# Dilated attention: products in pairs of units by seven block products, logits ahead of the products in each step

## The reference, cut to what matters

```
x = x + rms_norm(gmlp_mixer(rms_norm(x, pre[0])), post[0])
h = rms_norm(x, pre[1])
z = h @ w_in                      # q, k, v of 3 groups x 16 heads x 64, and a gate of 1024
for g, dilation in enumerate((1, 4, 16)):
    logits = q[g] @ k[g].T / 8 + bias      # each query sees keys at offsets 0, +-d .. +-64 d
    m, p, den = max, exp(logits - m), sum
    o[g], lse[g] = (p / den) @ v[g], m + log(den)
y = sum over g of softmax(lse)[g] * o[g]
x = x + rms_norm((y * silu(gate)) @ w_out, post[1])
```

## Time and profile before

| | |
|---|---|
| time, median of 3 runs | 3752.05 us (3745.39 to 3757.55) |
| the profiled execution | 3743.86 us, span 3742.3 us |
| PE busy | 3590.3 us (96%) |
| DVE busy | 1977.6 us (53%) |
| ACT busy | 1312.6 us (35%) |
| attention, from gmlp's last products to its own turns | 729 to 784 us |
| the 24 turns | from 784 us on; one of groups 0 and 1 takes 51.4 us, one of group 2 45.2 us |

### The profile page before, as it was taken

The page is one execution under the profiler, slowest core; times in us unless marked ns, Lnnn a source line. Parts: engine busy times, 40 slices in busy tenths (PEclk is TensorE's granted clock), DMA queues, the critical chain, the costliest instruction groups (busy, mean ns, idle before and its releaser), DMA issues. The chain is left out here.

```text
span 3742.3 us, 48660 instructions
## 1 busy us (share of the span) xinstructions
PE 3590.3 (96%) x18034; PEld 2903.4 (78%) x18034; DVE 1977.6 (53%) x3847; ACT 1312.6 (35%) x2559; POOL 112.2 (3%) x137
## 2 busy tenths in 40 slices
PE   8999999899999999999998899999978999999999
PEld 6878887777777777777777687777976877888887
DVE  5387773353334445555555544544675667754443
ACT  4254443333323333333223434444323323232222
POOL 0000001000000000000000100000000000000000
PEclk9999999999999999999999999999989999999999
DMA  4222226411111112111111330111323322233333
GB/s 147 91 102 97 93 89 217 146 62 50 59 59 58 54 59 62 58 49 47 48 46 51 113 110 24 43 43 64 101 92 100 102 82 82 77 113 99 96 96 121
DMA packets 140884, 308.87 MB, mean 83 GB/s; under 512 B 31936, under 2 KB 70384, under 8 KB 140576
## 3 DMA queue, kind: packets, MB, share of 16 engines
q1 hardware_dynamic: 123904, 264.81, 22.0%
q0 software_dynamic: 14688, 33.22, 3.0%
q10 hardware_dynamic: 2112, 8.39, 0.6%
HBM read 256.55 MB, written 56.04 MB: 84 GB/s over the span
## 5 line engine op out<-in xcount | busy, mean ns | idle before, releaser
L142 DVE TENSOR_TENSOR all_w_lo<-all_w_raw,all_w_hi 128x1024 fp32r<-128x1024 f32 x295 | 361.1, 1224 | 337.8 <-ACT all_w_hi L137 337.7
L137 ACT ACTIVATE all_w_hi<-all_w_raw 128x1024 fp32r<-128x1024 f32 x295 | 310.1, 1052 | 478.9 <-PE om_z L155 261.2
L1465 PE MATMUL da_z<-all_hi,all_w_hi 128*128 128x512 f32 x736 | 305.7, 415 | 4.1 <-DVE all_w_lo L142 4.1
L1465 PE MATMUL da_z<-all_hi,all_w_lo 128*128 128x512 f32 x736 | 291.1, 396 | 0.0
L1465 PE MATMUL da_z<-all_lo,all_w_hi 128*128 128x512 f32 x736 | 289.8, 394 | 0.0
L1326 ACT ACTIVATE da_pt<-da_tr 128x512 f32<-128x512 f32 (+1 forms) x192 | 101.0, 526 | 485.7 <-PE da_tr L1518 485.7
L155 PE MATMUL om_z<-all_hi,all_w_hi 128*128 128x512 f32 x640 | 257.3, 402 | 7.9 <-DVE all_w_lo L142 4.7
L1334 ACT ACTIVATE at_p<-at_logit,da_pair_max 128x256 f32<-128x256 f32 (+1 forms) x384 | 178.0, 465 | 239.1 <-DVE da_pair_max L1720 238.7
L155 PE MATMUL om_z<-all_hi,all_w_lo 128*128 128x512 f32 x640 | 255.8, 400 | 0.0
L155 PE MATMUL om_z<-all_lo,all_w_hi 128*128 128x512 f32 x640 | 253.7, 396 | 0.0
L155 PE MATMUL pr_g<-all_hi,all_w_hi 128*128 128x344 f32 (+1 forms) x624 | 211.7, 339 | 10.7 <-issue 4.9
(11 more groups left out here) (692 smaller groups left out, 7781.0 us busy)
## 6 DMA issues: line engine op xcount, KB each, us to landing
all_w_raw<-in_w_mlp SPq DMA_DIRECT2D x128, 512.0 KB, 3.5
all_w_raw<-in_w_ug SPq DMA_DIRECT2D x48, 512.0 KB, 4.1
all_w_raw<-in_w_qkv SPq DMA_DIRECT2D x48, 512.0 KB, 3.7
all_w_raw<-in_w_in SPq DMA_DIRECT2D x27, 512.0 KB, 3.6
da_w_raw<-in_w_qkv SPq DMA_DIRECT2D x24, 512.0 KB, 3.6
all_w_raw<-in_w_bo SPq DMA_DIRECT2D x24, 512.0 KB, 3.5
all_w_raw<-in_w_v SPq DMA_DIRECT2D x20, 512.0 KB, 4.6
vhat<-ag_vst ACTq DMA_DIRECT2D x4, 2048.0 KB, 7.3
```

The lines of the kernel that those rows point to most:

```text
L137: self.nc.scalar.activation(self.hi[b][:, :], self.raw[b][:, :], ACT.Copy).then_inc(self.hi_done[b], 1)
L142: self.nc.vector.tensor_tensor(self.lo[b][:, :], self.raw[b][:, :], self.hi[b][:, :].bitcast(F32), ALU.subtract).then_inc(self.lo_done[b], 1)
L1465: last = nc.tensor.matmul(z[h][:, :], wp[u][:, ws], ap[:, kk, cols], start=(kk == 0 and m == 0), stop=(kk == KT - 1 and m == 2))
```

## The change

- **Products.** Units go in 38 pairs: q and k of a turn, v of two turns, two units of the gate. Class `Seven` makes a pair as 7 blocks of 12 products each (`ORDER`, `PRODUCTS`), 84 where two units had 96. The first four units (q and k of pair 0, v of pairs 0 and 1) stay as they were (192 products).
- **Weights of a block.** a11, a12, a21, a22 are 128 x 512 quarters of the pair's weights, each loaded by a DMA of its own; s1 to s4 are sums of them (DVE: `add_lower`, `add_left`, `add_three`, `add_four`). Each of the seven is split into one of four ring slots, three blocks ahead of its use: `split_hi(n+3)` on ACT waits until block n-1 has been multiplied, `split_lo(n+3)` on DVE waits for it.
- **Combination.** Four PSUM banks bx, by, bz, bv hold block products. ACT copies bx and bz to `n2`, `n3` and writes the first quarter; DVE forms n2, n3 and the other three quarters, of q, k and v in strided order.
- **`block_work(n)`.** On DVE it is `split_lo(n+3)` and, by n mod 7: 4: `add_lower`, `add_left`, n2, n3 and quarter c22; 5: c21; 6: `add_three`; 0: `add_four` and c12; 1, 2, 3: nothing more. It stands in the step in which block n begins, ahead of DVE's copies of v (s = 0) and its bias pass. On ACT it stands ahead of the copy of the turned p and the exponentials.
- **Order on PE.** Of a step the logits of tile s-1 come first, then the products, then transposes of p, then p times v. The v transposes of s = 0 stand behind the first half-block. The logits of tile 0 wait for DVE's v copies too.
- **Shares.** Steps get half-blocks of 6 products: `full`, 21 a turn; turn 1 `short`, 21 with 8 in its step 0; turn 24 two in each step; 25 half-blocks follow the turns.
- **Norm and copies.** h is normalised before it is multiplied, so no quarter is scaled by `inv` on leaving PSUM; q and k have two buffers and are not copied. `tr` and `pv` have one PSUM bank each instead of two.
- **Start.** The first half of tokens of the new x, its norm, and its split are made in gmlp's out phase (`next_x`, `next_square`, `next_norm`, `next_hi`, `next_lo`); the other half in attention.
- **Other moves.** Biases are loaded at s = 9 of the turn before; the results of group 2 go to DRAM by POOL as those of group 1 do, and come back after the turns, where `turn_y` now runs; the gate's tanh and product follow there. Loops are written out instead of run with registers.

```diff
...
+                if KT + 1 <= n < KT + 5:
+                    for k in range(2 * (n - KT - 1), 2 * (n - KT)):
+                        next_x(k)
+                        if k:
+                            next_total(k)
+                if n >= KT + 6:
+                    for k in range(4 * (n - KT - 6), 4 * (n - KT - 5)):
+                        next_norm(k)
+                    next_lo(n - KT - 6)
...
+class Seven:
+    ORDER = ("a11", "s3", "s1", "s2", "a22", "a12", "s4")
+    N = 7
...
+    def load(self, sp, j, part, unit):
+        before = self.N * (j - 1)
+        wait(sp, self.lo_done, before + {"a21": 2, "a11": 4, "a22": 5, "a12": 6}[part])
+        if part in ("a11", "a12"):
...
+    def add_lower(self, dve, j):
+        t = self.tile
+        self.landed(dve, j, "a21")
+        self.landed(dve, j, "a22")
...
+    def add_left(self, dve, j):
+        t = self.tile
+        self.landed(dve, j, "a11")
+        dve.wait_ge(self.summed, 4 * j + 1)
+        self.plus(t["s3"], t["a11"], self.scales[j], t["a21"]).then_inc(self.summed, 1)
...
+    def split_hi(self, act, n):
+        j, i = divmod(n, self.N)
+        name = self.ORDER[i]
+        if name in self.loaded:
...
+        else:
+            act.wait_ge(self.summed, 4 * j + {"s1": 1, "s3": 2, "s2": 3, "s4": 4}[name])
+        wait(act, self.multiplied, n - self.slots + 1)
+        self.nc.scalar.activation(self.hi[n % self.slots], self.tile[name], ACT.Copy,
+                                  scale=self.scales[j] if name in ("a11", "a12") else 1.0).then_inc(self.hi_done, 1)
+    def split_lo(self, dve, n):
...
+    def products(self, out, n, block, start, ks):
+        b = n % self.slots
+        for k in ks:
+            cols = slice(k * P, k * P + P)
+            for m, (wp, ap) in enumerate(((self.hi, block[0]), (self.lo, block[0]), (self.hi, block[1]))):
+                last = self.nc.tensor.matmul(out, wp[b][:, cols], ap[:, k, :], start=start and k == 0 and m == 0,
+                                             stop=k == KT // 2 - 1 and m == 2, skip_group_check=True)
+        return last
...
+        PRODUCTS = (("b11", bx, True), ("t3", bz, True), ("t1", bv, True), ("t2", by, True), ("t4", bz, False), ("b21", bx, False), ("b22", bv, False))
...
+        full, short = (2, 2, 2, 2, 1, 2, 2, 1, 2, 2, 1, 2), (8, 2, 2, 1, 1, 1, 1, 1, 1, 1, 1, 1)
+        share_of = {n: short if n == 1 else (2,) * SUB if n == turns else full for n in range(1, turns + 1)}
+        at, work = 0, {}
+        for n in range(1, turns + 1):
+            for s in range(SUB):
+                work[n, s] = range(at, at + share_of[n][s])
+                at += share_of[n][s]
...
+            for n in range(1, turns + 1):
+                for s in range(SUB):
+                    for blk in begun(work[n, s]):
+                        block_loads(blk)
...
+            def block_work(n):
+                if n + 3 < NB:
+                    seven.split_hi(act, n + 3)
+                j, r = divmod(n - 1, Seven.N)
...
+                if r == 0:
+                    wait(act, s_c12, j)
+                    act.wait_ge(seven.multiplied, n)
+                    nc.scalar.activation(n2, bx[:, :], ACT.Copy).then_inc(s_xc, 1)
+                if r == 1:
...
+                if r == 5:
+                    free_to_leave(act, j, 0)
+                    act.wait_ge(seven.multiplied, n)
+                    out, view = dest(j, 0, 0)
+                    nc.scalar.activation(out, view(bx[:, :]), ACT.Copy).then_inc(s_c11, 1)
...
+                    nc.scalar.activation(den[:, 0, :, :], den[:, 0, :, :], ACT.Ln).then_inc(s_dln, 1)
                 for s in range(SUB):
-                    if bg and s == 0:
...
+                    for blk in begun(work[n, s]):
+                        block_work(blk)
+                    if 3 <= s < 3 + tiles:
...
-                        nc.scalar.activation(pt[t % 2][:, 0:wd], tr[t % 2][:, 0:wd], ACT.Copy).then_inc(s_pt, 1)
-                    if ag is not None and 1 <= s < 1 + tiles:
...
+            def gemm(x):
+                n, half = divmod(x, 2)
+                j, i = divmod(n, Seven.N)
+                name, out, start = PRODUCTS[i]
+                if half == 0:
+                    pe.wait_ge(seven.lo_done, n + 1)
+                    if i < 4 and j == 0:
...
+                    for sem, count in (((s_c11, j),), ((s_c21, j),), ((s_c12, j),), ((s_n2, j),), ((s_zc, j + 1),), ((s_xc, j + 1),), ((s_c22, j + 1),))[i]:
+                        wait(pe, sem, count)
...
+                last = seven.products(out[:, :], n, blocks[name], start, range(2 * half, 2 * half + 2))
+                if half == 1:
+                    last.then_inc(seven.multiplied, 1)
...
-                        turn_y(n - 2 - B_PAIRS, tiles * n)
                     if 1 <= s < 1 + tiles:
...
-                            pe.wait_ge(s_qs, n)
-                            if bg == 2:
...
                         wait(pe, s_max, c)
                         k0 = t * P + (WINDOW if ag == 2 else 0)
...
-                            last = nc.tensor.matmul(qk[hh][:, 0:wd], q[hs, t * P:t * P + P],
-                                                    k_[hs, k0:k0 + wd], start=True, stop=True)
+                            last = nc.tensor.matmul(qk[hh][:, 0:wd], q[a % 2][hs, t * P:t * P + P],
+                                                    k_[a % 2][hs, k0:k0 + wd], start=True, stop=True)
                         last.then_inc(s_qk, 1)
+                    for x in work[n, s][0:1 if s == 0 else None]:
+                        gemm(x)
+                    if s == 0:
+                        values_ready(pe, a)
+                        wait(pe, s_pt, tiles * a)
...
+                            last = nc.tensor.transpose(dst[:, (m % 4) * P:(m % 4) * P + P], v_new[a % 2][:, off + m * P:off + m * P + P], ident)
+                        last.then_inc(s_vt, 1)
+                        for x in work[n, s][1:]:
+                            gemm(x)
...
-                        wait(pe, s_pt, c - 1)
+                        wait(pe, s_pt, c)
...
-                                last = nc.tensor.transpose(tr[t % 2][:, i * P:i * P + P], p[t % 2][:, hh, x * P:x * P + P], ident)
...
-                        wait(pe, s_o, c - 1)
+                        wait(pe, s_o, c)
...
+            def block_work(n):
+                if n + 3 < NB:
+                    seven.split_lo(dve, n + 3)
+                j, r = divmod(n + 4, Seven.N)
...
+                    if r == 1:
+                        seven.add_lower(dve, j)
+                        seven.add_left(dve, j)
+                    if r == 3:
+                        seven.add_three(dve, j)
+                    if r == 4:
+                        seven.add_four(dve, j)
+                j, r = divmod(n - 1, Seven.N)
+                if n < 1:
...
+                if r == 3:
+                    dve.wait_ge(s_xc, j + 1)
+                    dve.wait_ge(seven.multiplied, n)
+                    nc.vector.tensor_tensor(n2, n2, by[:, :], ALU.subtract).then_inc(s_n2, 1)
+                    dve.wait_ge(s_zc, j + 1)
+                    dve.wait_ge(s_n2, j + 1)
+                    nc.vector.tensor_tensor(n3, n3, n2, ALU.add).then_inc(s_n3, 1)
...
+                    dve.wait_ge(s_n3, j + 1)
+                    out, view = dest(j, 1, 1)
+                    if second > 0:
+                        nc.vector.tensor_tensor(out, view(bv[:, :]), view(n3), ALU.add).then_inc(s_c22, 1)
...
+                if r == 4:
+                    dve.wait_ge(seven.multiplied, n)
+                    out, view = dest(j, 1, 0)
+                    if second > 0:
+                        nc.vector.tensor_tensor(out, view(bz[:, :]), view(n2), ALU.add).then_inc(s_c21, 1)
...
+                if r == 6:
+                    free_to_leave(dve, j, 0)
+                    dve.wait_ge(seven.multiplied, n)
+                    out, view = dest(j, 0, 1)
+                    nc.vector.tensor_tensor(out, view(bv[:, :]), view(n2), ALU.add).then_inc(s_c12, 1)
...
                 for s in range(SUB):
-                    u = s // 4
-                    if g is not None and s % 4 == 0:
-                        if u < 2:
-                            w.split_lo(dve, u + 1, n)
...
-                    if g is not None and s % 2 == 1:
-                        leave(n, g, s, z[(s // 2) % 2][:, :])
-                    if g is None and s % 2 == 1:
-                        h = (s // 2) % 2
...
+                    for blk in begun(work[n, s]):
+                        block_work(blk)
                     if s == 0:
                         dve.wait_ge(s_vt, n)
                         wait(dve, s_pv, tiles * a)
-                        nc.vector.tensor_copy(v[:, 0:4, :], tr[0][:, :].rearrange("p (m c) -> p m c", c=P))
-                        last = nc.vector.tensor_copy(v[:, 4:8, :], tr[1][:, :].rearrange("p (m c) -> p m c", c=P))
```

(94 more changed lines are left out.)

942 lines of the change are left out of this document (559 added, 383 removed).

## The result

The changed kernel takes 3907.6 us (median of 4 runs, 3895.26 to 3908.62) against 3750.29 us, a ratio of 1.041 (95% interval 1.0383 to 1.0438): slower, as forecast, but by 157 us where the forecast had 78, and outside the range of 3720 to 3890.

A forecast was written before the change was run, and what follows sets the result against it. PE's products were taken to bound the kernel, with new waits before logits: 3743.9 - 105.3 (products) + 176 (round trips) + 16 (clock) - 9 (start) = 3822, plus 8 for the median, 3830 us; range 3720 to 3890.

The forecast's parts named there:

- What bounds the kernel, and what is removed: PE's products set each turn; 456 fewer save 105.3 us, leaving 47.2 us a turn by PE alone in groups 0 and 1.
- The round trip through `block_work`: Logits, ACT's split_hi, DVE's block work, bias pass, next logits: 2.5 + W or 3.85 + W us; waits sum to +176 us.
- the front end: Round trip from logits at L to DVE's start of block work, put at L+1.6 us.
- step 4 of odd turns: Block work of residue 4 there takes 4.0 us; the next logits wait 3.0 us.
- Even borders: At the start of even turns, tile 0's logits wait 3.9 us in group 0, 4.45 in groups 1 and 2.
- The clock: PE's lower clock after long idle: twelve even borders at 1.3 us each, +16 us, between 0 and 30.
- Single banks: One PSUM bank each for `tr` and `pv`: costed at nothing; if ACT is late, up to 0.5 us a step.
- Rival (d): PE's clock falls at each of some 66 waits over 1.4 us: 82 us in place of 16, about 3896 us; chance 0.08.
- The start: Before turn 1: -15 us from less PE idle, +6 for uneven turn 1; together -9 us, between -20 and +10.
- The tail: After the turns, where `turn_y`, tanh and products of the gate meet: 0 us, between -10 and +10.
- gmlp's out phase: Half of x made there, about 24 us more of DVE and ACT: costed at nothing; without cover up to 24 us.
- VectorE: DVE Perf Modes: By this page residue 4's six DVE operations would take 0.3 us more, the whole some 12 us more; the trace disagreed.

The follow-up runs named there:

- Kernel 10: kernel 9 with the shares of kernel 6 (22 half-blocks in odd turns, 20 in even): 3656.23 us, 0.9753 of the kernel before.
- (1): Changed kernel with DVE's block work moved behind the bias pass of its step, in step 0 behind the v copies: 3708.15 us, 0.9883 of the kernel before.
- (3): Changed kernel with the logits of each step behind its product blocks on PE, DVE and ACT as they were: 3704.71 us, 0.9867 of the kernel before.
- (5): Changed kernel with the edits of (1) and (3) at once: 3686.35 us, 0.9823 of the kernel before.
- (4): Changed kernel with one more unused DVE sum of 128x512 in each block work of residue 4: 3922.94 us, 1.046 of the kernel before.
- kernels 1 to 3: (1), (3) and, between them, the changed kernel with only split_lo left ahead of the bias pass, sums and quarters behind it: 3748.09 us (0.9995).
- kernel 6: Changed kernel with other shares alone, 22 half-blocks in odd turns and 20 in even, every block begun with its step: 3814.84 us (1.0154).
- kernel 9: (5) with add_lower and add_left a block earlier, from block work of residue 4 to residue 3: 3669.2 us, 0.9781 of the kernel before.

## Why the prediction was right or wrong

- **What bounds the kernel, and what is removed**: right. Kernel 10 gets the 47.2 us a turn in group 0.
- **The round trip through `block_work`**: right in place, releaser and sum (178.7 us in turns 1 to 23; forecast 176 for turns 2 to 24), shown by taking it away on DVE (1), on PE (3) and on both (5), and by making it 0.41 us longer (4). Within it, the front end was 0.64 us too short, most of it ACT's copy of the turned p, and step 4 of odd turns therefore 3.7 to 4.3 us instead of 3.0. Even borders were right to 0.7 us. By groups the forecast had 45, 63 and 68 us for turns 2 to 24; PE's idle times before logits sum to 49, 62 and 64.
- **The clock**: the step that failed. "So waits under 3 us go free by these rows and the twelve even borders (3.9 to 4.5 us) do not", 16 us, "between 0 and 30". It came to 53.1 us in 23 turns. Three things were wrong. The eleven waits at step 4 of odd turns are over 3.5 us and one more stands in turn 24, so there are 24 long waits in place of 12; shorter ones are not all free; and a long one costs more than the 1.3 us of the forecast. After the wait of 3.68 us in turn 5, products stand 0.43 us apart, at a granted clock of 0.50 (1041.4 to 1045.8), and 2.0 us are lost:

```profile
1041.99 0.63 PE L1214 MATMUL da_bz<-nb_t_hi,all_w_lo 128*128 128x512 f32 x1
...
1043.70 0.63 PE L1214 MATMUL da_bz<-nb_t_lo,all_w_hi 128*128 128x512 f32 x1
```

  I counted PE's idle times of over 0.6 us in the changed kernel, from turn 2 on, against the slow products behind them. All 24 of 3.5 us and more are followed by some, 1.7 us lost in the mean (1.0 to 2.2); of 21 between 1.5 and 3.5 us ten are, with 0.6 to 1.8 us; of 32 below 1.5 us none. "Free" had rested on a single row (2.80 us of idle, no loss). Rival (d) had taken 1.24 us for all 66 waits: too many; its 82 us lie 29 above the measured 53, the forecast's 16 lie 37 below. Its sign, a granted clock under 0.95 through the turns, is there in part: 0.95 in group 0, 0.94 and 0.92 behind (790 to 1200, 1200 to 1660, 1660 to 2090 us). That its total of 3896 us is nearer to the measured 3908 than the forecast is no point for it, as other terms that both left out fill the difference. In kernels 1 to 3, with few long waits left, slow products are 12 to 16 us in 23 turns: the clock follows the waits and is no cost of its own.
- **Single banks, "costed at nothing"**: wrong, 16.3 us. "Wanted again a step later, over 3.5 us" is true, but o, the reader, stands behind the block work on DVE. I bounded it by ACT's lateness and not by what is queued ahead of the reader on DVE. It was small only as PE was late itself: with PE's waits taken away (5) it doubled.
- **The start**: the near match of -8.6 and -9 is luck. PE reached turn 1 at 787.8 us and not by 770 to 780, so the start gained 8.6 us of the 15 forecast; turn 1 then took 58.3 us against 47.2 of PE's own work, 11 us where +6 was forecast, and these stand in the lines of the waits. **The tail**: 14 us more than its products, 11.0 of it turn 24's waits before logits, of which the sum of 176 was to hold 8.5. **gmlp's out phase**: hidden, as said; its end lies between 729.0 and 731.5 us in the changed kernels' profiles, 729.1 before.
- **VectorE: DVE Perf Modes** of the Trainium skill, "The DRAIN you can't avoid", has the next operation start only when the pipe of the one before is empty. The same section adds "A next op that is not held starts earlier", which the prediction left out when it set the page against the rows. By the timeline above, operations that wait for nothing start 0.61 us apart (1035.22, 1035.83), which agrees with that addition. Those that wait for the one before start 0.79 apart, where the section found no extra cost for a semaphore between two operations. The six took 4.20 us, near the 4.3 worked out from the page's duration, but as a mixture of these two distances. The measurement decides.
- **The ledger**: 3822 forecast for the profiled execution against 3907. Of the 85 us, 37 are the clock in turns 1 to 23, 16 the bank of p times v, 14 turn 24 and the tail, 11.5 the spread of executions in untouched stages, the rest (6) small terms. With 53 us for the clock in place of 16 the forecast would have been 3867 us, inside its range. The range ended at 3890, as it took the clock at 30 at most and left no room for terms costed at nothing to come together.

## What to carry to other kernels

When two engines hand a small thing back and forth once a step, what counts is where the hand-over stands in each queue, not how busy the engines are: put the big independent work (the products here) between the two sides of it on both, and check each reader of a single buffer for what is queued ahead of it. The same 456 products less gave +4.1% with both on one side, -1.2 to -1.3% with one side put right and -2.5% with both, the work spread and aligned. Price an idle time of TensorE with the slow products that follow it, and take the frequency from more than one row.

## What the runs showed of the hardware

- The same wait can cost clock or not. In the changed kernel no idle time of PE of 0.6 to 1.5 us did (32), all above 3.5 us did (24), and ten of the 21 between; in kernel 6 all three of 0.6 to 1.5 us (1.46 us each) stand ahead of slow products, and 19 of 31 between 1.5 and 3.5. In kernel 9 turns 11 and 13 have 1.2 and 1.5 us of slow products behind idle times of 2.16 and 2.03 us, and turn 15, with 2.02 us, none. What decides it beside the length is open.
- An operation put between two dependent ones made DVE's block work 0.41 us longer (4.20 to 4.61 in experiment 4), while independent operations of this size start 0.60 to 0.61 us apart and dependent ones 0.79: it fills in part a gap that was there.
- The recurrence stage, unchanged, runs at a granted clock of 0.74 to 0.86 and takes 77.5 to 85.1 us from one execution to another: more than one change in these runs was worth.
